# Six query and key projections of the first block computed with the head dimensions on partitions

## The reference, cut to what matters

```python
def apply_rotary(t, cos, sin):
    t1, t2 = jnp.split(t.astype(jnp.float32), 2, axis=-1)      # halves of one head's 64 dimensions
    return jnp.concatenate([t1 * c - t2 * s, t1 * s + t2 * c], axis=-1)
...
proj = jnp.einsum('bsd,de->bse', xn, w_in)
q_a, k_a, v_a, q_r, k_r, v_r, g_r, gate_logits = jnp.split(proj, IN_SPLIT_POINTS, axis=-1)
q_a = apply_rotary(...); k_a = apply_rotary(...)
for g, (window, dilation) in enumerate(((128, 1), (512, 4), (2048, 16))):
    o, l = dilated_window_attention(q_a[:, :, g], k_a[:, :, g], v_a[:, :, g], dilation, ...)
q_r = apply_rotary(...); k_r = apply_rotary(...) * (RET_QK_DIM ** -0.5)
```

## Time and profile before

| | |
|---|---|
| Median of 3 runs | 2770.03 us (2769.05 to 2770.14) |
| Span of the profiled execution, first to last instruction | 2767.8 us (its own run time isn't given beside it; the span is 2.2 us under the median) |
| PE busy (matmul) | 2611.3 us, 94% of the span |
| DVE busy | 1219.5 us, 44% |
| ACT busy | 880.0 us, 32% |
| POOL busy | 853.0 us, 31% |
| Chain that ended last, by engine | PE 68%, DMA 23%, DVE 5%, ACT 2%, POOL 1%, issue 1% |

### The profile page before, as it was taken

The page is one execution under the profiler, slowest core; times in us unless marked ns, Lnnn a source line. Parts: engine busy times, 40 slices in busy tenths (PEclk is TensorE's granted clock), DMA queues, the critical chain, the costliest instruction groups (busy, mean ns, idle before and its releaser), DMA issues.

```text
span 2767.8 us, 36753 instructions
## 1 busy us (share of the span) xinstructions
PE 2611.3 (94%) x14332; PEld 1851.6 (67%) x14332; DVE 1219.5 (44%) x2420; ACT 880.0 (32%) x1671; POOL 853.0 (31%) x1166
## 2 busy tenths in 40 slices
PE   9999999999988888888888899999999999999999
PEld 7888777888433333333333367788888887888887
DVE  6433745225643333333333357553441565644422
ACT  4433335322211111111111144553332446433332
POOL 5343434552000000000000043345555435345554
PEclk9999999999999999999999999999999999999999
DMA  4233122336999999999999951122332221123322
GB/s 163 75 105 105 67 76 77 104 122 253 414 428 427 429 428 428 428 429 429 428 429 427 426 184 68 43 92 92 95 115 94 90 100 61 62 91 107 106 92 76
DMA packets 128151, 571.99 MB, mean 207 GB/s; under 512 B 11152, under 2 KB 58640, under 8 KB 102928
## 3 DMA queue, kind: packets, MB, share of 16 engines
q1 hardware_dynamic: 122768, 560.82, 51.0%
q10 hardware_dynamic: 5248, 9.32, 1.1%
HBM read 565.86 MB, written 4.26 MB: 206 GB/s over the span
## 4 chain that ended last, share of the span: by engine, by line
PE 68%; DMA 23%; DVE 5%; ACT 2%; issue 1%; POOL 1%; SPq 0%; ACTq 0%; POOLq 0%; DVEq 0%
PE ps L392 42%; DMA wide<-in_moe_w 17%; PE ps L1577 8%; DMA arena<-in_moe_w 5%; PE ps L2098 4%; PE ps L2077 2%; PE ps L2067 1%; PE ps L2118 1%; PE ps L673 1%; PE ps L708 1%; PE ps L689 1%; PE ps L2084 1%; POOL ring_r L349 1%; PE ps L1353 1%; PE ps L937 0%
## 5 line engine op out<-in xcount | busy, mean ns | idle before, releaser
L349 POOL TENSOR_TENSOR ring_r<-ring,ring_r 128x256 fp32r<-128x256 f32 (+2 forms) x1136 | 834.3, 774 | 1819.2 <-ACT ring_r L332 1819.2
L392 PE MATMUL ps<-xnT_r,ring_r 128*128 128x512 f32 (+1 forms) x1664 | 484.0, 374 | 0.0
L392 PE MATMUL ps<-ring_r,xnT_r 128*128 128x512 f32 (+1 forms) x1296 | 412.5, 389 | 3.0 <-DVE xn_r L3164 2.5
L392 PEld LDWEIGHTS ps<-xnT_r,ring_r 128*128 128x128 f32 x1664 | 304.5, 188 | 56.5 <-issue 1.3
L392 PE MATMUL ps<-ring_r,arena_r 128*128 128x512 f32 x1392 | 325.3, 392 | 0.3 <-POOL ring_r L349 0.3
L392 PE MATMUL ps<-xn_r,ring_r 128*128 128x512 f32 (+1 forms) x832 | 310.2, 373 | 0.0
L332 ACT ACTIVATE ring_r<-ring 128x1024 fp32r<-128x1024 f32 (+2 forms) x284 | 272.0, 1025 | 89.8 <-DMA ring<-in_w_down 67.9
L392 PEld LDWEIGHTS ps<-ring_r,arena_r 128*128 128x128 f32 x1392 | 260.7, 188 | 57.7 <-issue 2.8
L392 PEld LDWEIGHTS ps<-ring_r,xnT_r 128*128 128x128 f32 x1296 | 250.8, 200 | 49.9 <-issue 5.7
L2098 PE MATMUL ps<-wide,arena 128*32 128x512 f32 x752 | 192.4, 658 | 93.4 <-DMA wide<-in_moe_w 93.4
L2098 PEld LDWEIGHTS ps<-wide,arena 128*32 128x32 f32 x752 | 53.3, 118 | 230.7 <-issue 230.7
(11 more groups left out here) (407 smaller groups left out, 3491.0 us busy)
## 6 DMA issues: line engine op xcount, KB each, us to landing
wide<-in_moe_w SPq DMA_DIRECT2D x143, 2048.0 KB, 32.9
arena<-in_moe_w SPq DMA_DIRECT2D x46, 2048.0 KB, 32.9
ring<-in_w_in SPq DMA_DIRECT2D x22, 2048.0 KB, 8.3
ring<-in_w_up SPq DMA_DIRECT2D x20, 2048.0 KB, 8.5
ring<-in_w_down SPq DMA_DIRECT2D x10, 2048.0 KB, 7.7
ring<-in_w_in SPq DMA_DIRECT2D x16, 512.0 KB, 4.8
ring<-in_w_out SPq DMA_DIRECT2D x4, 2048.0 KB, 8.3
ring<-in_w_ret_branch SPq DMA_DIRECT2D x2, 2048.0 KB, 8.7
```

Source lines behind the costliest of these rows:

```text
L349: ins = nc.gpsimd.tensor_tensor(ring_r[:, q % 2, piece], ring[:, q % 2, piece], ring_r[:, 2 + q % 2, piece].bitcast(F32), ALU.subtract)
L392: ins = nc.tensor.matmul(bank, left, right, start=(start and k == 0), stop=(stop and k == 2))
```

## The change: what it does

Every q and k job but those of unit 0 (group 1's queries) and of the retention's keys is "crossed": group 1's keys, queries and keys of groups 2 and 0, and the retention's queries, 24 jobs. Its stationary operand is 128 columns of the weights and its moving one all 512 tokens, so a job makes two heads' dimensions on partitions for every token. Its rotation needs the other half of each head, which now lies 32 partitions away. ACT copies the four quarters of 32 partitions from PSUM to `swapped`, each to its partner's place (`swap_crossed_act`); DVE multiplies that by the signed sines, the job's output by the cosines, and adds the two into `qT` or `kT` (`rotate_crossed_dve`). The rot entry of these jobs, with its four transposes and ACT's copy, is gone, and with it its turn of the three banks. Tables of cosine and sine by dimension and token are 0.5 MB, loaded by SP ahead of weight unit 1 into `rows[:, 3]`. Several waits count the new semaphores. Cut to its core:

```diff
+    turns = (np.arange(S, dtype=np.float32)[None] * np.tile(inv, P // inv.size)[:, None]).astype(np.float32)
+    signs = np.where(p % DH < DH // 2, -1.0, 1.0)
+    parts["rope_t"] = np.concatenate([np.cos(turns), signs * np.sin(turns)], 1)
...
+        rope_loaded, halves_swapped, rotated = rel_loaded, stage_sems["x_kept"], stage_sems["x_low"]
...
+            swapped = (tmp, lay(BANK))
...
+            cos_T, sin_T = rows[:, 3, 0:S], rows[:, 3, S:]
...
+                self.crossed = [n for n, job in enumerate(jobs) if job[3] == CROSSED]
+                self.roped = [n for n, job in enumerate(jobs) if job[0] != "v" and n not in self.crossed]
+                self.by_dve = sorted(self.roped + self.crossed)
...
-            jobs = [(kind, base + j, i, tokens(i, False)) for j, kind in enumerate("qk") for i in range(NT)]
+            jobs = [(kind, base + j, i, tokens(i, False) if base + j == 0 else CROSSED) for j, kind in enumerate("qk") for i in range(NT)]
...
-            jobs = [(kind, U_REST + j, i, tokens(i, False)) for j, kind in enumerate("qvkv") for i in range(NT)]
+            jobs = [(kind, U_REST + j, i, CROSSED if kind == "q" else tokens(i, False)) for j, kind in enumerate("qvkv") for i in range(NT)]
...
-                    ins = products(ps[:, dense_bank(e), :], [tokens_of(x, toks, c) for x in range(2)], [w[:, c, :] for w in chunks_of_unit(u)],
-                                   start=(c == 0), stop=(c == KC - 1))
+                    flags = dict(start=(c == 0), stop=(c == KC - 1))
+                    if toks == CROSSED:
+                        ins = products(ps[:, dense_bank(e), :], [xnT_high[:, c, :], h_low[:, c, :]], [w[:, c, i * P:(i + 1) * P] for w in chunks_of_unit(u)],
+                                       weights_left=True, **flags)
+                    else:
+                        ins = products(ps[:, dense_bank(e), :], [tokens_of(x, toks, c) for x in range(2)], [w[:, c, :] for w in chunks_of_unit(u)], **flags)
...
+                        pe.wait_ge(rotated, M.crossed0)
...
+                    if n in M.crossed:
+                        rotate_crossed_dve(v, M, k[0], n)
...
+        def rotate_crossed_dve(v, M, e, n):
+            x = M.crossed.index(n)
+            y = M.crossed0 + x
+            kind, _, b, _ = M.jobs[n]
+            way = "qk".index(kind)
+            rot, swapped = X.rot[:, x % 2, :], X.swapped[y % 2]
+            v.wait_ge(Z.proj_ready, M.jobs0 + n + 1)
+            if y == 0:
+                v.wait_ge(rope_loaded, 16)
+            v.wait_ge(Z.turned, M.rots0 + sum(r < n for r in M.roped) - (x == 0))
+            v.wait_ge(halves_swapped, y + 1)
+            nc.vector.tensor_tensor(swapped, swapped, X.sin_T, ALU.mult)
+            nc.vector.scalar_tensor_tensor(out=rot, in0=ps[:, dense_bank(e), :], scalar=M.scales[way], in1=X.cos_T, op0=ALU.mult,
+                                           op1=ALU.mult).then_inc(Z.taken_dve, 1)
+            v.wait_ge(Z.taken_dve, M.dves0 + M.by_dve.index(n) + 1)
+            dst = M.heads[way][:, b, :]
+            if M.permuted:
+                rot, swapped = (z.rearrange("p (k r) -> p r k", r=STRIDE) for z in (rot, swapped))
+                dst = dst.rearrange("p (r k) -> p r k", r=STRIDE)
+            nc.vector.tensor_tensor(dst, rot, swapped, ALU.add).then_inc(rotated, 1)
+            v.wait_ge(rotated, y + 1)
+        def swap_crossed_act(a, M, e, n):
+            y = M.crossed0 + M.crossed.index(n)
+            scale = M.scales["qk".index(M.jobs[n][0])]
+            a.wait_ge(Z.proj_ready, M.jobs0 + n + 1)
+            if y >= 2:
+                a.wait_ge(rotated, y - 1)
+            elif y == 0:
+                a.wait_ge(Z.roped, M.rots0 + len(M.roped))
+            half = DH // 2
+            for at in range(0, P, half):
+                other = at ^ half
+                ins = nc.scalar.activation(X.swapped[y % 2][at:at + half], ps[other:other + half, dense_bank(e), :], ACT.Copy, scale=scale)
+            ins.then_inc(halves_swapped, 1)
...
+                            a.wait_ge(rotated, M.crossed0 + len(M.crossed))
...
+                    elif c == KC - 1 and M.entries[e][1] in M.crossed:
+                        swap_crossed_act(a, M, e, M.entries[e][1])
+                        if M.before is None and M.entries[e][1] == 2 * NT - 1:
+                            decays_act(a, 1)
...
-            pool.wait_ge(rel_loaded, 16)
+            pool.wait_ge(rel_loaded, 32)
...
+            at, n = TABLES["rope_t"]
+            sp.dma_start(rows[:, 3], const[:, at:at + n]).then_inc(rope_loaded, 16)
```

More of the change, by code:

```diff
@@ L589, in build @@
             probs = lay(2, BANK)
+            swapped = (tmp, lay(BANK))
+            assert lay.at <= 15104
             lay.at = 15104
@@ L612, in build @@
         FIRST_HALF, SECOND_HALF, WHOLE = slice(0, HALF), slice(HALF, P), slice(0, P)
-        ENDS = "ends"
+        ENDS, CROSSED = "ends", "crossed"
         end_tokens = extra_r[:, 0:2 * KC * P].rearrange("p (x c t) -> p x c t", x=2, c=KC)
@@ L814, in __init__ @@
                 self.rots0 = before.rots0 + len(before.roped) if before else 0
-                self.acts0 = before.acts0 + len(before.jobs) - len(before.roped) if before else 0
+                self.acts0 = before.acts0 + len(before.jobs) - len(before.by_dve) if before else 0
+                self.dves0 = before.dves0 + len(before.by_dve) if before else 0
+                self.crossed0 = before.crossed0 + len(before.crossed) if before else 0
                 self.jobs, self.permuted, self.scales, self.values = jobs, permuted, scales, values
@@ L818, in __init__ @@
                 self.attention, self.first, self.apart, self.leaves, self.merges = attention, first, apart, leaves, merges
-                self.roped = [n for n, (kind, _, _, _) in enumerate(jobs) if kind != "v"]
+                self.crossed = [n for n, job in enumerate(jobs) if job[3] == CROSSED]
+                self.roped = [n for n, job in enumerate(jobs) if job[0] != "v" and n not in self.crossed]
+                self.by_dve = sorted(self.roped + self.crossed)
                 self.entries = []
@@ L880, in taken @@
                     eng.wait_ge(Z.out_kept, k + 1)
-                elif k in self.roped:
-                    eng.wait_ge(Z.taken_dve, self.rots0 + self.roped.index(k) + 1)
+                elif k in self.by_dve:
+                    eng.wait_ge(Z.taken_dve, self.dves0 + self.by_dve.index(k) + 1)
                 else:
-                    eng.wait_ge(Z.taken_act, self.acts0 + k - sum(r < k for r in self.roped) + 1)
+                    eng.wait_ge(Z.taken_act, self.acts0 + k - sum(r < k for r in self.by_dve) + 1)
             def bank_taken(self, eng, bank):
@@ L966, in mixer_dve @@
                     n = M.entries[k[0]][1]
[L967 to L980, removed]
+                    if n in M.crossed:
+                        rotate_crossed_dve(v, M, k[0], n)
+                    elif n in M.roped:
+                        m = M.roped.index(n)
+                        v.wait_ge(Z.proj_ready, M.jobs0 + n + 1)
+                        if M.rots0 + m >= 2:
+                            v.wait_ge(Z.turned, M.rots0 + m - 1)
+                        rope(ps[:, dense_bank(k[0]), :], X.tmp, X.rot[:, m % 2, :], cos[:, m % NT], sin[:, m % NT], HEADS)
+                        v.wait_ge(Z.taken_dve, M.dves0 + M.by_dve.index(n) + 1)
+                        nc.vector.tensor_tensor(X.rot[:, m % 2, :], X.rot[:, m % 2, :], X.tmp, ALU.add).then_inc(Z.roped, 1)
+                        v.wait_ge(Z.roped, M.rots0 + m + 1)
+                    if M.before is None and n == 0:
                         start_low_dve(v, NT - 1)
-                    elif M.before is None and m < 2 * NT - 1:
+                    elif M.before is None and n < 2 * NT - 1:
                         next(decays)
-                    if M.merges and m >= NT:
-                        i = m - NT
+                    if M.merges and n in M.roped:
+                        i = m
                         v.wait_ge(Z.exp_ready, 2)
@@ L1023, in mixer_act @@
                         n = M.entries[e][1]
-                        j = n - sum(r < n for r in M.roped)
+                        j = n - sum(r < n for r in M.by_dve)
                         dst = M.values[j]
@@ L1035, in mixer_act @@
                         nc.scalar.activation(dst, ps[:, dense_bank(e), :], ACT.Copy).then_inc(Z.taken_act, 1)
+                    elif c == KC - 1 and M.entries[e][1] in M.crossed:
+                        swap_crossed_act(a, M, e, M.entries[e][1])
+                        if M.before is None and M.entries[e][1] == 2 * NT - 1:
+                            decays_act(a, 1)
                 elif what == "rot":
                     m = M.entries[k][1]
+                    way = "qk".index(M.jobs[M.roped[m]][0])
                     a.wait_ge(Z.turned, M.rots0 + m + 1)
-                    dst, src = M.heads[m // NT], ps[:, dense_bank(k), :]
```

(10 more changed lines are left out.)

## The result

The changed kernel takes 2789.28 us (median, 2788.83 to 2789.64) against 2769.54 for the kernel before beside it: a ratio of 1.0071, 95% interval 1.0059 to 1.0084. It is slower by 19.7 us; forecast was 2772.8 in a range of 2762 to 2781. Its profiled span is 2787.8 us, 20.0 more than before's, and all of it arises in the first block: the last matmul of the first block (line 1577 before, 1636 after) starts at 697.6 us against 676.9, 20.7 later, and from there to the end both take some 2090 us (2090.2 and 2090.9).

The account below looks back on a forecast made before the run. It took PE to bound the first block: -10.6 of transposes, +2 x (2.4 + 1.6) + 3.6 + 0.8 of waits, +0.2 + 0.8 of small terms gave +2.8 us, so 2772.8 us, in a range of 2762 to 2781.

Parts of the forecast that it names:

- What is removed: In 24 jobs of the first block, PE loses the rot entry's four transposes, 0.44 us each: -10.6 us.
- What is swapped at no cost: In the 24 jobs, 576 matmuls exchange stationary and moving operands: 0 us, either way 0.7; table load 0, at worst 1.2.
- The swap: On ACT, four 32-partition activations 0.48 us apart take 2.0 us, +1.45 a job; bounds 0.6 and 2.35.
- 11 us of waits for each us: Groups 2 and 0 and the retention: PE's waits grow 11 us per us of swap, until they reach zero.
- Places A and B: Queries (A) and keys (B) of groups 2 and 0: PE waits for ACT's copy 2.4 and 1.6 us, each twice.
- Place C: The retention's queries: later high halves, rotation, masks and exponentials make PE wait 3.6 us.
- Place D: Retention, "values" of pair 2: DVE's lateness uses up 3.5 us of bank slack; 0 to 1.5 us, taken as 0.8.
- Banks: Group 2's first job waits 0.7 us for its bank; 0.7 goes at the head of the rest; sum 0.
- Small terms: Strided adds of groups 1 and 2, 0.2 us; handovers, clashes and DVE's doubled two-operand work in SBUF, 0.8 us.
- any new wait of PE is paid in full: First block, 30 to 385 us: PE is the bound, with only 1.2 us of waits, so new waits count fully.
- the delay feeds itself: Rival, ACT's list in query jobs: non-overlapping swaps or slow DVE, then late POOL; about +8, 2778 us; chance 0.29.

Follow-up runs that it names:

- the run of fewer pieces: Changed kernel with each swap as one 128-partition activation or two of 64, halves not exchanged: 2765.91 us and 2774.16 us.
- the two halves: Changed kernel with each swap made as two activations of 64 partitions, each to its own partitions, halves not exchanged: 2774.16 us, ratio 1.0018 to before.
- the one copy: Changed kernel with each swap made as one activation of 128 partitions, halves not exchanged: 2765.91 us, ratio 0.9989 to before.

## Why the prediction was wrong

The sign, the engine and the places were right: PE lost at "back" of tiles 0 and 2 of both attentions and in the retention more than the transposes gave. Two terms of the sum failed.

- **What is removed** (-10.6) held: 32 transposes of that line are left of 128, and every account above closes with it.
- **What is swapped at no cost** held within what the accounts leave over: none needs a term for the exchanged operands.
- **The swap, 2.0 us, is the first failed term.** It is 2.38 to 2.40. I took 0.48 as the distance between two copies from one pair of full-height rows; the pieces of a swap start 0.60 apart. What the part ahead of the prediction says of any two instructions that follow at once, an overlap of some 0.1 us, isn't so for these. The upper bound of 2.35, "if they don't overlap", was nearly the truth. By "11 us of waits for each us" this is +4.3 us, and in the run of fewer pieces the law was 13 to 14 with the clock in it.
- **Places A and B** with the right price: A 2.4 + 2 x 0.39 = 3.2, measured 3.42 and 3.09; B 1.6 + 0.78 = 2.4, measured 3.60 and 2.51. Place C 3.6 + 3 x 0.39 = 4.8, measured 1.91 and 1.25 = 3.2, at two tiles instead of one, and 1.2 more at "turn" just ahead, where the same late exponentials show. All five together 16.0 against 15.8 measured. The way of reckoning, idle ahead of the copy against what is put in front of it, was sound.
- **Place D** 0.8: none of it seen. **Banks**: the +0.7 came (line 1088), and the 0.7 that should have gone did go. **POOL** 1.7 us, of which 1.5 are in group 1 ahead of all attention, a place where I had looked for nothing. There its 16 pieces start at 55.30 instead of 53.69 and take 13.36 us instead of 11.63.
- **Small terms**: the strided add takes 1.06 us at 104.50 and 1.57 at 119.37, beside POOL; in line it takes 0.69 by itself and 1.05 beside POOL (line 978 at 108.87 before). So the stride costs 0.4 to 0.5 where I took 0.2. The Trainium skill's rule on strided float32 ("SBUF — State Buffer", Door 1: The DMA port swizzle) stood nearer than my row, as this trace has it.
- **The halved clock is the second failed term, and the larger: 11.8 us, forecast 0.** It isn't named anywhere in the prediction. The step that failed is "any new wait of PE is paid in full": a wait was priced at its length, and each of the five places cost 1.6 to 3.1 us more than its waits. The rival "the delay feeds itself" had its condition met (it decides from a swap of 2.25) and its direction right, but its mechanism, POOL's ring late in groups 2 and 0, hardly shows: the ring's waits there and in the retention come to 0.2 us. It came to 2778. With the swap at 2.39 the sum gives +7.1 (2777), and with the clock +18.9, which is the result within 1 us. That it comes so close is luck in part: B and the turn at C came out longer than reckoned, and POOL in group 1 was not in the sum, while "back" at C and D came out shorter.

Its possibility could have been read in the trace before. The mean clock of 0.989 hides it, and the first block has 1.00 throughout, but in the experts' stage PE waits 37 times for 2 us or more for weights, and behind 17 of these waits the clock falls. Before's timeline and windows at two neighbouring places (PE, and the granted clock behind the count):

```profile
1098.01 3.63 PE L2098 MATMUL ps<-wide,arena 128*32 128x512 f32 x16 [2.76 <-DMA wide<-in_moe_w]
1112.69 5.32 PE L2098 MATMUL ps<-wide,arena 128*32 128x512 f32 x16 [2.76 <-DMA wide<-in_moe_w]
```
```profile
1096.00:1098.00 2.00, 0.00 (x0) 1.00 0.96 410
1098.00:1100.00 2.00, 2.00 (x10) 1.00 1.06 451
1100.00:1102.00 2.00, 2.00 (x12) 1.00 1.02 434
1110.00:1112.00 2.00, 0.00 (x0) 1.00 0.98 418
1112.00:1114.00 2.00, 1.31 (x7) 1.00 1.04 442
1114.00:1116.00 2.00, 2.00 (x8) 0.50 0.98 418
```

Two waits of 2.76 us: behind the second the clock is 0.50 and the same 16 matmuls take 5.32 us, behind the first it stays at 1.00 and they take 3.63. So these rows would have given the lower clock a chance, about one in two, at each wait of that length, and not a certainty; what decides between the two isn't shown. There the chain of waits runs along the DMA; in the first block it runs along PE.

## What to carry to other kernels

Count pieces, not partitions: an activation of 32 partitions costs what one of 128 does (0.59 us each), and four in a row didn't overlap. When a wait of some 2 to 3 us lands on the engine that is the bound, look in the same trace for what its clock does behind such waits elsewhere, and how often, and price both. And where work is moved to an engine with room, its place in that engine's order can decide more than its amount: the same change cost 20 us in one order and came out 3 us below before in another, which these runs call no change.

## What the runs showed that I had not expected

- Pieces of 32 partitions start 0.60 us apart, crossed or not, and last 0.589 each. Full-height copies and high halves start 0.1 us before the one ahead of them ends, but next to a piece of 32 or 64 partitions they don't: in the changed kernel the high halves at 143.54 start when the swap begun at 141.13 has ended (2.39 us).
- PE's clock fell to 1.2 GHz with every wait of 2.4 us or more between 30 and 400 us in these kernels, and with some shorter ones: in the changed kernel where two stops of 0.33 and 0.86 us followed each other, in the two halves behind 1.69 us, in the one copy not behind 1.97. In the experts' stage it fell at 17 of 37 waits of 2.09 to 3.07 us. Filling the waits with products that nobody reads was worth 5 us although it added 5.2 us to the path.
- A program that differs only in the first block lost 6.7 us near 1620 us, in an issue that nothing in the profile explains.
